# Prompt attention of a sparse-attention layer: transposes and their copies placed one quarter of a step later

## The reference

```
lw = einsum('ntghd,nkgd->ntghk', qg, kw) + bw     # scores with relative-position bias
pw = masked_softmax(lw, mw[:, None, None, :])     # causal softmax
ow = einsum('ntghk,nkgd->ntghd', pw, vw)          # weighted values
o = gt[..., 0:1] * oc + gt[..., 1:2] * osel + gt[..., 2:3] * ow
```

## Time and profile before

| what | value |
|---|---|
| median of three runs | 2561.54 us |
| the profiled execution, its own time | 2560.77 us |
| its span in the profile | 2559.1 us |
| mean granted TensorE clock, share of full speed | 0.963 |
| PE busy over the span | 2338.8 us (91%) |
| PE weight loads (PEld) busy | 1754.0 us (69%) |
| DVE busy | 1060.6 us (41%) |
| ACT busy | 577.2 us (23%) |
| POOL busy | 1039.7 us (41%) |

### The profile page before, as it was taken

The page is one execution under the profiler, slowest core; times in us unless marked ns, Lnnn a source line. Parts: engine busy times, 40 slices in busy tenths (PEclk is TensorE's granted clock), DMA queues, the critical chain, the costliest instruction groups (busy, mean ns, idle before and its releaser), DMA issues. The chain is left out here.

```text
span 2559.1 us, 38344 instructions
## 1 busy us (share of the span) xinstructions
PE 2338.8 (91%) x15282; PEld 1754.0 (69%) x15282; DVE 1060.6 (41%) x1957; ACT 577.2 (23%) x1328; POOL 1039.7 (41%) x912
## 2 busy tenths in 40 slices
PE   6999799789999999999996999999998989999997
PEld 4776444456777777667775778677785767777775
DVE  2001777344430242367886545363543044302412
ACT  1001566321000000135553323232420010000000
POOL 1331345245654464465653131121215456534640
PEclk9999899799999999999998999999998999999998
DMA  6632100451211221211125020110202212112110
GB/s 242 211 106 89 33 1 1 160 191 66 82 62 71 83 82 66 112 66 50 66 70 54 6 100 6 48 54 21 84 6 103 90 64 78 66 66 99 66 66 38
DMA packets 49947, 193.74 MB, mean 76 GB/s; under 512 B 15650, under 2 KB 24610, under 8 KB 33522
## 3 DMA queue, kind: packets, MB, share of 16 engines
q1 hardware_dynamic: 45922, 175.76, 20.1%
q0 software_dynamic: 3856, 15.61, 2.0%
HBM read 170.80 MB, written 28.81 MB: 78 GB/s over the span
## 5 line engine op out<-in xcount | busy, mean ns | idle before, releaser
L1498 PE MATMUL ps<-hid,ring 128*128 128x288 f32 x768 | 194.8, 410 | 23.1 <-DVE hid L1594 23.1
L1498 PE MATMUL ps<-xn,ring 128*128 128x288 f32 x768 | 201.9, 412 | 8.9 <-DVE xn L1578 8.4
L1498 PEld LDWEIGHTS ps<-hid,ring 128*128 128x128 f32 x768 | 146.4, 191 | 64.8 <-DVE hid L1594 24.9
L1498 PEld LDWEIGHTS ps<-xn,ring 128*128 128x128 f32 x768 | 146.5, 192 | 53.4 <-issue 8.0
L1524 ACT ACTIVATE p<-ps 128x288 f32<-128x288 f32 x48 | 19.7, 411 | 631.5 <-PE ps L1498 631.5
L218 PE MATMUL ps<-xn,ring 128*128 128x288 f32 x640 | 157.7, 410 | 2.8 <-ACTq L562 2.8
L1562 POOL TENSOR_TENSOR prod<-prod,rstd 128x1152 f32<-128x1152 f32 x32 | 83.8, 2620 | 179.9 <-DVE prod L1640 163.3
L218 PEld LDWEIGHTS ps<-xn,ring 128*128 128x128 f32 x640 | 122.9, 192 | 37.2 <-ACTq L562 2.9
L2747 PE MATMUL ps<-xn,ring 128*128 128x288 f32 x512 | 138.3, 416 | 3.6 <-PE ps L2812 3.6
L1498 PE MATMUL ps<-x_sum,wsum 128*128 128x288 f32 x512 | 134.1, 416 | 3.2 <-DVE x_sum L1581 2.5
L744 POOL TENSOR_SCALAR ring<-ring,fac 128x128 f32<-128x128 f32 (+2 forms) x96 | 92.2, 976 | 103.2 <-DVE fac L976 103.2
(11 more groups left out here) (449 smaller groups left out, 4806.8 us busy)
## 6 DMA issues: line engine op xcount, KB each, us to landing
ring<-in_w_mlp SPq DMA_DIRECT2D x64, 1024.0 KB, 4.9
ring<-in_w_gdn_in SPq DMA_DIRECT2D x16, 1024.0 KB, 4.9
ring<-in_w_nsa_in SPq DMA_DIRECT2D x10, 1024.0 KB, 8.3
ring<-in_w_gdn_z SPq DMA_DIRECT2D x8, 1024.0 KB, 4.9
x<-in_seq_state SPq DMA_DIRECT2D x4, 2048.0 KB, 8.6
out_seq_state<-x SPq DMA_DIRECT2D x4, 2048.0 KB, 11.2
ring<-in_w_gdn_out SPq DMA_DIRECT2D x8, 1024.0 KB, 5.7
out_win_old<-in_win_rows POOLq DMA_DIRECT2D x1, 8064.0 KB, 47.4
```

The lines of the kernel that those rows point to most:

```text
L1498: mm = nc.tensor.matmul(S.ps[:, base + BANK[p], 0:HT], stationary(p, blk.units[pair // 4], pair % 4), moving(blk.kind, p, pair), start=pai ...
```

## The change

The groups of transposes on PE and their copies on ACT stand one slot later: group g is now in slot g + 1, so slot 0 has none and slot 3 has group 2. Within a slot the order stays. No instruction is added or removed; `chunk_no`, which only numbers the groups, is as before, because their relative order is.

```diff
@@ -832,8 +832,8 @@
                 for s in range(PT):
                     if step < NJ:
                         qk(step, s)
-                    if s < 3 and 0 <= step - 2 < NJ:
-                        turn(step - 2, s)
+                    if s > 0 and 0 <= step - 2 < NJ:
+                        turn(step - 2, s - 1)
                     if 0 <= step - 3:
                         times_v(step - 3, s)
@@ -890,8 +890,8 @@
-                    if s < 3 and 0 <= step - 2 < NJ:
-                        turned_copy(step - 2, s)
+                    if s > 0 and 0 <= step - 2 < NJ:
+                        turned_copy(step - 2, s - 1)
```

## The result

The changed kernel takes **2593.84 us** (median of 4 runs, 2588.16 to 2594.65) against 2561.69 us before (median of 4, 2554.99 to 2562.17). The ratio is 1.0116, 95% interval 1.0100 to 1.0132: slower by 32.2 us. The forecast was 2592 us, 31.5 us more than the profiled execution.

A forecast was written before the change was run, and what follows sets the result against it. The bound was taken to be a ring of waits through PE, DVE and ACT, 23.43 us a pair, not one full engine. Longer ring +20.5, ends 0, clock falls +11 make 31.5 on 2560.77: 2592 us, range 2576 to 2606.

The forecast's parts named there:

- The bank's copy: PE's stops between groups: each group starts when ACT has copied the previous group's first half, 0.76 or 0.63 us after copies begin.
- Points 1 and 2: PE's order: earlier tile 1 scores gain 0; DVE's stop for tile 2's scores goes, part of 25.5 us.
- Point 3: ACT copies group 0 behind tile 1's late exponential, so group 1 waits on PE; even-step gap some 3.0 us.
- Point 4: ACT copies group 2 behind the step's last exponential, so L804 waits for a bank on PE, some 2.2 us.
- The ring: Waits through PE, DVE and ACT: 9.71 plus 16.65, 26.36 us a pair against 23.43, seven times: +20.5 us.
- The clock: PE: one fall to half clock per pair at the smaller price, 12.6 us, less 1.6 for one already there: +11 us.
- the other gap: PE's gap ahead of group 1 in even steps, some 3.0 us; a clock fall behind it priced at 1.8 us.
- The ends: Two steps without scores at the end and first two without groups: 0, between -3 and +3 us.
- The first link: Stage's start: first two steps without groups at 0, full ring counted from step 3, seven times in all, +20.5 us.
- The total: Whole kernel: 20.5 + 0 + 11 = 31.5 us on 2560.77, giving 2592 us.
- PE as the bound: Rival: PE's busy time binds and its new gaps fill with work it had anyway; 2561 us, chance 0.07.
- the clock that holds: Rival: PE's clock doesn't fall behind the new gaps, leaving 20.5 us alone; 2581 us, chance 0.28.

The follow-up runs named there:

- filler in the gap: Changed kernel plus 16 unused transposes of constants on PE ahead of L804 in steps 3 to 15: 2578.60 us, ratio 1.0069.
- that run: Changed kernel with compressed transposes L804, products L824 and copies L885 moved from the end of odd steps into slot 0: 2562.87 us, ratio 1.0005 to the kernel before.
- both gaps filled: Changed kernel plus 16 unused transposes ahead of L804 in odd steps and 20 ahead of group 1 in even steps from step 6: 2584.64 us, ratio 1.0089.
- the 20.92 us pair: From the kernel before with only PE's groups a slot later and compressed L804, L824, L885 in slot 0 of odd steps: 2537.12 us, ratio 0.9909.

## Why the prediction was right

- *The bank's copy, not POOL, ends PE's stops.* Right. PE starts 0.74 us after the copies of group 0 begin and 0.63 after those of group 2 (forecast 0.76 and 0.63). The profile again names POOL's L744 for the 0.87 us at 392.35, although POOL's program is the same in all these kernels and only the place of the copies moved the stops.
- *Points 1 and 2, PE's side costs nothing, DVE's stop for tile 2's scores goes.* Right in sign: alone it is the 4 us of gain. The stop doesn't vanish in the changed kernel: in the odd step it is 0.52 us at 391.52 instead of 1.09, in the even step 1.24 instead of 1.16; tile 3's grows from 1.05 to 1.83 us.
- *Point 3, group 0's copies.* In odd steps it is a stop of 0.87 us. The 3.0 us forecast for the even steps are not in the changed kernel: of the six even steps behind a stop of L804, group 1 waits 0.45 and 0.54 us in two and not at all in four, where group 2 waits 0.45 to 0.60. The fall behind L804 makes PE slow just there, and its work fills the gap. With that fall gone (filler in the gap) the stop is 2.44 us; 3.0 was 0.6 too much.
- *Point 4, L804.* Right: 2.22 us (forecast 2.2), seven times. Without the stop the loss is gone within the measurement, with the reservation made at that run.
- *The ring of 9.71 and 16.65, 26.36 a pair.* With both gaps filled and no fall 9.79, 16.61 and 26.40. This term, +20.5 us, stands. In the changed kernel the short part is 10.1 to 10.8 us, though the clock is 1.00 in the one at 383.7 to 393.9 us; why was not traced.
- *The clock, one fall a pair at 1.6 to 1.8 us.* Right in kind: one fall a pair, behind L804's gap. 27.94 - 26.40 is 1.54 us; one pair of the five paid 3.1. But the sum took the price of the other gap (1.8) for it; for L804's the prediction had 2.1. Both were too high, as a fall behind the other gap costs 1.1 to 1.4 us (the pairs of 27.5 to 27.8 with one filler). And the fall already there before, put at 1.6 us, cost 0.5 (a pair of 23.94 instead of 23.43). The errors nearly cancel: the five pairs lost 23.7 us where 4.5 each make 22.5.
- *The ends at 0.* These hold. The 2.2 us before step 2 are not the change's. The 3.6 us at the end are those of the seventh stop of L804, which the sum had counted among its seven: with that gap filled the end takes 18.7 us, before 18.3.
- *The first link* is what was mis-sized. Only one of the seven stops of L804 lies before the first `out_copy`, worth 4.5 us, and steps 2 to 5 lost 9.2: 1.7 up to tile 3's scores of step 3, and 7.5 from there to those of step 5. There the clock is 0.62 over 311 to 329 us, which makes some 13.7 us of half clock where a pair like that at 369 us (27.9 us at 0.88) has some 6.7. Why this fall lasted longer was not tested.
- *The total* owes something to luck. The stage lost 38.7 us, not 31.5. The profiled executions differ by only 33.9 because later stages took 4.7 less, which the sum didn't have and which the change doesn't explain.
- *Rivals.* PE as the bound fell with the 20.92 us pair; the clock that holds fell with the rows at 0.55 and with the filler.

## What to carry to other kernels

In a pipeline written out by hand over several in-order engines, first find what really ends each wait, then write down the ring of links with durations from one period of the trace; here that gave the period at full clock to 0.1 us before anything ran (26.36 for 26.40), and the clock had to be added. Moving a producer and its consumer later together isn't neutral: the order on the copying engine sets when a bank comes free, and the consumer should be given distance from the copy it needs, as the fastest version does. A link's price depends on what follows it, so parts of a reordering must be weighed together.

## What the runs showed of the hardware

Each of the seven idle gaps of 2.2 us on PE in the changed kernel is followed by about 7 to 14 us at half clock, although PE has hardly a stop then (9.00 of 9.00 us in 399 to 408 us). Putting 2.0 us of useless transposes into the gap took the fall behind it away and made the kernel 12 us faster by the ratios. Gaps of 0.87 us were not followed by one. Falls came without a gap too: at 426 us before, and near 391 us with both gaps filled.

A fall also hides a later gap, as slow matmuls fill it: with half clock behind L804 the even step shows stops of 0.45 to 0.60 us, with full clock there one of 2.44. Filling one gap then moved the fall to the other.
